# Out projection run once for each half of the tokens in a fused encoder layer

## What is computed

```python
def layer(h, attend, conv_state, w_in, w_out, ...):
    ...
    mix = jnp.concatenate([group_rms_norm(attn, g_attn_out, HEAD_DIM),
                           group_rms_norm(gate_b * conv_y, g_conv_out, CONV_GROUP)], axis=-1)
    h = h + rms_norm(jnp.einsum('bte,ed->btd', mix, w_out), g_post_mix)
    xf = rms_norm(h, g_pre_ffn)
    ff = jax.nn.silu(jnp.einsum('btd,df->btf', xf, w_gate)) * jnp.einsum('btd,df->btf', xf, w_up)
    h = h + rms_norm(jnp.einsum('btf,fd->btd', ff, w_down), g_post_ffn)
```

## Time and profile before

| what | us |
|---|---|
| median of 3 runs | 2453.63 (2452.96 to 2456.07) |
| profiled execution, its own time | 2450.74 |
| span in its trace | 2449.0 |
| TensorE busy | 2374.5 (97%) |
| VectorE busy | 1541.6 (63%) |
| ScalarE busy | 1011.0 (41%) |
| GpSimd busy | 81.9 (3%) |

### The profile page before, as it was taken

One profiled execution on the slowest core, in us unless ns is written; L12 is line 12 of the kernel. 1 busy time (PEld: TensorE's weight loads), 2 busy tenths in 40 slices (PEclk: granted clock), 3 DMA queues, 4 the chain that ended last, 5 costly groups with the idle time before them and its releaser, 6 DMA issues.

```text
span 2449.0 us, 42232 instructions
## 1 busy us (share of the span) xinstructions
PE 2374.5 (97%) x18280; PEld 2334.6 (95%) x18280; DVE 1541.6 (63%) x1778; ACT 1011.0 (41%) x1245; POOL 81.9 (3%) x143
## 2 busy tenths in 40 slices
PE   8999999999999996699999999999999899999998
PEld 7999999999999995699999999999999899999998
DVE  5323333343434225877777777777777688888887
ACT  6345444432333223444444444444444333333346
POOL 0000000000002110000000000000000000000002
PEclk9999999999999998799999999999999999999999
DMA  7222322222324331234445444444445666645562
GB/s 234 84 75 70 97 77 79 74 87 87 87 81 146 99 104 73 75 130 133 154 135 168 136 154 149 132 155 134 154 134 168 246 210 231 231 143 156 183 204 87
DMA packets 325916, 327.93 MB, mean 134 GB/s; under 512 B 8508, under 2 KB 282324, under 8 KB 325604
## 3 DMA queue, kind: packets, MB, share of 16 engines
q1 hardware_dynamic: 299264, 275.57, 35.9%
q10 hardware_dynamic: 26468, 49.67, 5.5%
HBM read 264.20 MB, written 61.00 MB: 133 GB/s over the span
## 4 chain that ended last, share of the span: by engine, by line
PE 90%; DVE 5%; DMA 2%; ACT 2%; issue 1%; SPq 0%; POOL 0%; ACTq 0%; DVEq 0%; POOLq 0%
PE ps L955 37%; PE ps L438 30%; PE ps L1012 17%; PE ps L722 4%; DMA ff_lo_scr<-hid_lo 2%; PE ps L666 1%; DVE xs L1800 1%; DVE t_lo L1778 1%; DVE misc L1804 0%; DVE panel L1792 0%; DVE wide L1768 0%; DVE misc L1772 0%; ACT xs L1350 0%; DMA panel<-in_w_down_dram 0%; DMA misc<-in_x_sample_dram 0%
## 5 line engine op out<-in xcount | busy, mean ns | idle before, releaser
L955 PE MATMUL ps<-xs,t_hi 128*128 128x272 f32 x4928 | 940.6, 291 | 33.0 <-DVE xs L1800 19.1
L955 PEld LDWEIGHTS ps<-xs,t_hi 128*128 128x128 f32 x4928 | 781.1, 190 | 34.6 <-issue 32.2
L955 PE MATMUL ps<-xs,t_lo 128*128 128x272 f32 x2464 | 716.8, 291 | 0.0
L1778 DVE TENSOR_TENSOR t_lo<-panel,t_hi 128x1024 fp32r<-128x1024 f32 (+1 forms) x405 | 485.5, 1199 | 228.3 <-ACT t_hi L1343 225.3
L1343 ACT CAST t_hi<-panel 128x1024 fp32r<-128x1024 f32 (+1 forms) x405 | 413.4, 1021 | 455.1 <-PE ps L1012 241.9
L1012 PE MATMUL ps<-xd,t_hi 128*128 128x272 f32 x2464 | 470.4, 290 | 14.3 <-DVE y_left L1949 8.2
L955 PEld LDWEIGHTS ps<-xs,t_lo 128*128 128x128 f32 x2464 | 467.3, 190 | 0.0
L438 PE MATMUL ps<-act_hi,w_hi 128*128 128x272 f32 (+1 forms) x2048 | 435.4, 294 | 3.1 <-DVE act_lo L1615 1.9
L438 PE MATMUL ps<-act_lo,w_hi 128*128 128x272 f32 (+1 forms) x2048 | 426.9, 290 | 0.0
L438 PE MATMUL ps<-act_hi,w_lo 128*128 128x272 f32 (+1 forms) x2048 | 426.5, 289 | 0.0
L1012 PEld LDWEIGHTS ps<-xd,t_hi 128*128 128x128 f32 x2464 | 390.7, 190 | 15.5 <-issue 15.4
(11 more groups left out here) (183 smaller groups left out, 1728.4 us busy)
## 6 DMA issues: line engine op xcount, KB each, us to landing
w_raw<-in_w_in_dram SPq DMA_DIRECT2D x96, 512.0 KB, 3.8
panel<-in_w_up_dram SPq DMA_DIRECT2D x44, 1024.0 KB, 5.6
panel<-in_w_gate_dram SPq DMA_DIRECT2D x43, 1024.0 KB, 5.1
panel<-in_w_down_dram SPq DMA_DIRECT2D x32, 1024.0 KB, 5.9
ff_hi_scr<-hid_hi SPq DMA_DIRECT2D x22, 952.0 KB, 4.5
ff_lo_scr<-hid_lo SPq DMA_DIRECT2D x22, 952.0 KB, 7.4
w_raw<-in_w_out_dram SPq DMA_DIRECT2D x32, 512.0 KB, 3.9
xd<-ff_hi_scr ACTq DMA_DIRECT2D x28, 544.0 KB, 8.0
```

The source lines that it names most:

```text
L955: mm = nc.tensor.matmul(out, w[:, k, :], xs[:, x, part, k, :], start=begins and k == 0 and w is hi and part == 0, stop=k == KH - 1 and w i ...
L1778: V.tensor_tensor(tile_of(t_lo, i), raw_tile(i), tile_of(t_hi, i).bitcast(F32), ALU.subtract)\
```

## The change

The out projection runs once for tokens 0 to 271 and then once for tokens 272 to 543. Every weight tile of w_out is loaded, cast and split twice (64 tiles), and a tile now serves 24 matmuls. The split mix lies in new buffers by half (`mx_hi`, `mx_lo`); the second half's is made while the first pass runs (`mix_high_late`, `mix_rest_late`). Output chunks use one of four banks in turn. While the second pass runs, the first half's norm, residual, squares and second norm are made, and A11 and A12 are split. The squares of h of the first half are folded by VectorE from 16 chunks to one ahead of one matmul; ScalarE's queue stores h. At the end of the second pass four products whose inputs are of the first half (B11 and B21 of steps 0 and 1) are made, with weight tiles that come through the ring of w_out as tiles 64 to 67. Steps 0 and 1 skip these two products.

S1 and S2 get raw buffers of their own, and GpSimd makes S3 and S4; the sums are gated by `s_pool`. `xs` is a list with a new order in memory (`XS_AT`), since S1's and S4's places overlap buffers that must be free first, and `xd` slots are permuted alike (`XD_AT`). In the down projection the last pair's first product goes into the gate buffer, VectorE's wait for the earlier store comes after the rest of B22 of its first step, the last pair's sums, rounding and rest move, and its store comes ahead of a panel load.

```diff
-    OUT_T = 2 * KC
+    OUT_T = 4 * KC + 4
...
+        mx_hi, mx_lo = ([sb_at(f"mx_{part}{t}", 17408 * (2 * p + t), [P, KC, TH], F32R) for t in range(2)]
+                        for p, part in enumerate(("hi", "lo")))
+        XS_AT = {A11: 0, A12: 2, S2: 1, S3: 3, S1: 4, A22: 5, S4: 6}
+        xs = [sb_at(f"xs{x}", 17408 * XS_AT[x], [P, 2, KH, TH], F32R) for x in range(7)]
+        s2_raw = sb_at("s2_raw", 69632, [P, KH, TH])
+        s1_raw = sb_at("s1_raw", 112640, [P, KH, TH])
...
+        XD_AT = [0, 1, 4, 5, 2, 3, 6, 7, 8, 9, 10, 11]
...
             sp.dma_start(resid, h_scr).then_inc(h_loaded, 16)
-            for q in range(2, KC // 2):
+            for q in range(2, KC):
                 load_out(q)
+            for k in range(PRE):
+                load((4, KC, T_OUT), k, gate_up[k // 2][:, TK * (k % 2):TK * (k % 2 + 1), 0:P])
...
+                if step == LAST + 3:
+                    store_hidden(FF // 2 - 1)
                 load_panel(step, 1)
-                if step > 3 and step % 2 == 0 and step // 2 - 2 < FF // 2:
+                if step > 3 and step % 2 == 0 and step // 2 - 2 < FF // 2 - 1:
                     store_hidden(step // 2 - 2)
...
+            for e in range(2, 2 * KC):
+                if e >= 4:
+                    pe.wait_ge(out_copied, e - 3)
+                if e == KC:
+                    pe.wait_ge(mix_late, 4)
+                for half in range(2):
+                    pe.wait_ge(lo_ready, T_OUT + 2 * e + half + 1)
+                    out_part(e, half, list(range(TK)))
+                if e == KC:
+                    out_sums(0)
+                if e == KC + 8:
+                    pe.wait_ge(h2_summed, 4)
+                    nc.tensor.matmul(ps[:, 5, 0:TH], neg1[:, :], h2_sq[0][:, 0, :], start=True, stop=True)\
+                        .then_inc(ms_ready, 1)
+            out_sums(1)
...
+            pe.wait_ge(ms_log, 3)
+            pre_product(0)
+            pre_product(1)
+            h2_sums(0)
+            pre_product(2)
+            for g in range(1, 4):
+                h2_sums(g)
+            pre_product(3)
...
+            for e in range(2 * KC):
+                t, n, q = e // KC, e % KC, e // 2
+                for half in range(2):
+                    ahead = 2 * e + half + LEAD
+                    if 2 * e + half >= 2 and ahead < OUT_T:
+                        round_weights((4, ahead // 4, T_OUT), ahead % 4)
+                if e in (3, 5, 7, 9):
+                    mix_high_late((e - 3) // 2)
+                if n == KC - 1:
+                    load_log_table(1)
+                act.wait_ge(chunk_done, CH_OUT + e + 1)
...
+                A(squares[n % 2][:, t * TH:(t + 1) * TH], ps[:, n % 4, 0:TH], ACT.Square).then_inc(sq_made, 1)
...
+            make_rstd(3)
+            for g in range(4):
+                square_stream(1, g)
+            load_log_table(2)
+            tile_high(ring(0, T2))
+            make_rstd(4)
+            act.wait_ge(product_done, PRE)
+            x_high(A22, x_block(KH, KH, 1), x_normed, 8)
+            x_high(S2, s2_raw[:, :, :], s_made, 2)
...
+                    act.wait_ge(xs_lo, 5)
+                    x_high(S1, s1_raw[:, :, :], s_pool, 2)
...
+                if e in (KC + 1, KC + 2):
+                    for g in range(2):
+                        scale_mix(0, 2 * (e - KC - 1) + g)
+                if e in (KC + 3, KC + 5):
+                    for g in range(2):
+                        add_mix(0, e - KC - 3 + g)
+                if e == KC + 7:
+                    fold_squares(0)
+                if e == KC + 8:
+                    for level in range(1, 4):
+                        fold_squares(level)
...
+            V.tensor_tensor(s1_raw[:, :, :], a21, a22, ALU.add).then_inc(s_made, 1)
+            dve.wait_ge(product_done, PRE)
+            dve.wait_ge(s_made, 1)
+            V.tensor_tensor(s2_raw[:, :, :], s1_raw[:, :, :], a11, ALU.subtract).then_inc(s_made, 1)
...
-                if step > 1:
+                if 1 < step < LAST:
                     dve.wait_ge(hid_stored, 32 * (step // 2))
...
+                if step == LAST:
+                    dve.wait_ge(hid_stored, 32 * (step // 2))
+                    dve.wait_ge(c12_up, FF // 2)
+                    V.tensor_copy(quarter(hid, 0, 1), quarter(gate, 0, 1))
...
+            pool.wait_ge(s_made, 1)
+            G.tensor_tensor(a21, a11, a21, ALU.subtract).then_inc(s_pool, 1)
+            pool.wait_ge(s_made, 2)
+            G.tensor_tensor(a12, a12, s2_raw[:, :, :], ALU.subtract).then_inc(s_pool, 1)
```

More of the change, by code:

```diff
@@ L945, in _, with out_part @@
-            mm.then_inc(ms_ready, 1)
+            def out_part(e, half, ks):
+                t, n = e // KC, e % KC
+                slot = (2 * e + half) % SLOTS
+                hi, lo = (w[:, slot, :].rearrange("p (k n) -> p k n", k=TK) for w in (w_hi, w_lo))
+                for k in ks:
+                    c = TK * half + k
+                    for w, part in ((hi, 0), (hi, 1), (lo, 0)):
+                        x = mx_lo[t][:, (c + 1) % KC, :] if part else mx_hi[t][:, c, :]
+                        mm = nc.tensor.matmul(ps[:, n % 4, 0:TH], w[:, k, :], x,
+                                              start=c == 0 and w is hi and part == 0,
+                                              stop=c == KC - 1 and w is lo, skip_group_check=True)
+                if ks[-1] == TK - 1:
+                    mm.then_inc((first_used, chunk_done)[half], 1)
@@ new lines, in _, with pre_product @@
+            out_sums(1)
+            def pre_product(k):
+                step, q = k // 2, k % 2
+                pe.wait_ge(lo_ready, T_OUT + 4 * KC + k + 1)
+                pe.wait_ge(xs_lo, 3 if q else 2)
+                pe.wait_ge(out_copied, 2 * KC)
+                hi, lo = (w[:, k, :].rearrange("p (k n) -> p k n", k=TK) for w in (w_hi, w_lo))
+                for c in range(KH):
+                    for w, part in ((hi, 0), (hi, 1), (lo, 0)):
+                        mm = nc.tensor.matmul(step_bank(step, "ac"[q]), w[:, c, :], xs[q][:, part, c, :],
+                                              start=c == 0 and w is hi and part == 0, stop=c == KH - 1 and w is lo,
+                                              skip_group_check=True)
+                mm.then_inc(product_done, 1)
@@ L963, in _ @@
                 for q in range(7):
-                    i = 7 * step + q
+                    if step < 2 and q <= B21:
+                        continue
+                    i = ring(step, q)
                     pe.wait_ge(tile_lo, i + 1)
@@ L1446, in _ @@
                     silu(quarter(gate, 1, 1), (c22_made, step + 1))
-                tile_high(ahead + 2)
+                tile_high(ring(step + 1, T2))
             def scale_chunk(c):
@@ new lines, in normalize, with x_rest @@
+            def normalize(t, c0, n):
+                for c in range(c0, c0 + n):
+                    x = resid[:, c, tokens_of(t)]
+                    last = V.scalar_tensor_tensor(out=x, in0=x, scalar=column(c + C_PREFFN), in1=rstd[:, tokens_of(t)],
+                                                  op0=ALU.mult, op1=ALU.mult)
+                last.then_inc(x_normed, 1)
+            def x_rest(x, made, block, k=0, n=KH):
+                dve.wait_ge(xs_hi, made)
+                V.tensor_tensor(xs[x][:, 1, k:k + n, :], block, xs[x][:, 0, k:k + n, :].bitcast(F32), ALU.subtract)\
+                    .then_inc(xs_lo, 1)
@@ L1775, in tile_rest @@
+            for ahead in range(4 * KC + LEAD, OUT_T):
+                rest_of_weights((4, ahead // 4, T_OUT), ahead % 4)
             def tile_rest(i):
@@ L1918, in _ @@
                     hidden_rest(step // 2 - 1)
-                tile_rest(7 * step + 6)
+                tile_rest(ring(step, B22))
                 if step == 0:
@@ L1923, in _ @@
                     c11(step)
-                tile_rest(ahead)
+                if step:
+                    tile_rest(ring(step + 1, B11))
                 combine(step + 1, T1)
@@ L1927, in _ @@
                 combine(step + 1, T2)
[L1928 removed]
+                if step:
+                    tile_rest(ring(step + 1, B21))
                 c21(step)
                 combine(step + 1, T3)
[L1931 removed]
+                tile_rest(ring(step + 1, T2))
             def take_down(d, q):
@@ L1985, in _ @@
                     combine(step + 1, T2)
-                    tile_rest(ahead + 1)
+                    tile_rest(ring(step + 1, B21))
                 take_down(d, T4)
@@ L1989, in _ @@
                     combine(step + 1, T3)
-                    tile_rest(ahead + 2)
+                    tile_rest(ring(step + 1, T2))
             take_down(DSTEPS - 1, B22)
```

416 lines of the change are left out of this document (217 added, 199 removed).

## The result

The changed kernel takes 2466.5 us (median of 5 runs, 2464.4 to 2470.1) against 2453.6 before (2453.0 to 2456.1): a ratio of 1.0053, 95% interval 1.0041 to 1.0065. It is 13 us slower, where 9.4 us faster was forecast. The measured time lies outside the range of 2424 to 2458.

What follows compares the result with a forecast made beforehand. TensorE, busy 97% of the span, was taken to bound the kernel. Out projection and transition +2.2, down projection -11.6, sum -9.4 on 2450.7: 2441.3, or 2444 as a median; range over all cases 2424 to 2458.

Steps and rivals of the forecast that it cites:

- supply term: Out projection, tiles 8 to 50: casts wait for loads through two raw slots, 6.5 us a pair against 6.05; +10.1.
- transition's sum: Out projection's end to steady products: 23.5 + 39.7 less products done and low clock, 52.6 us, gain -34.6.
- rival 1: Weights keep pace with TensorE in the out projection (at most 6.05 us a pair): 2425.7 us; chance 0.14.
- Start and load of h: Out projection's start costs +5.1 us; the load of h delays tile 8, costing +10.1.
- Rival 2: Inserted VectorE work adds in full to the out projection's weight supply loop: 17.8 us new, 2462 us; chance 0.13.
- Fold: TensorE waits behind chunk 24 of the out projection for VectorE's folded sums: +9.6 us (3.5 if weights run ahead).
- End to X: Out projection's end to the first half's second norm (X): last square at about 3.7 us, X at 23.5.
- X to steady products: Second norm's start to steady products: GpSimd's S3 and S4 at 7.0 us each, first product X + 17.4, end X + 39.5.
- Down projection: Its start: two TensorE holes shrink, together -11.6 us (-15 to -4).
- first hole: Down projection's start: VectorE no longer stands for an earlier hidden pair's store; -9.6 us, as little as -4.
- second hole: Down projection, two steps later: wait behind the last pair's store, now moved ahead of a panel load; -2 (bounds +5, -5).
- Rival 3: Down projection: the panel behind the store lands only at 2000, +4.9 instead of -2; 2451 us; chance 0.13.

Runs made afterwards that it cites:

- experiment 5: Changed kernel with a third raw slot for the out projection's weight tiles from tile 8 on: 2439.6 us, ratio 0.9942 to the kernel before.
- experiments 1 to 3: Changed kernel with S3 and S4 on VectorE: alone 2461.1 us; plus two unused GpSimd subtractions 2468.1; plus two unused GpSimd copies instead 2466.5.
- experiments 5, 7, 10: Changed kernel with third raw slot: alone 2439.6 us; with h in eight pieces 2428.2; with these, later fold matmul, S3/S4 on VectorE, store behind panel 2414.1.
- experiment 8: Kernel before with only the start of the down projection changed, the last pair's store ahead of the panel load: 2448.2 us, ratio 0.9975.
- experiment 9: Kernel before with only the start of the down projection changed, the last pair's store behind the panel load: 2441.9 us, ratio 0.9956.

## Why the prediction was wrong, step by step

The forecast of -9.4 and the profiled +15.8 are 25.2 apart. The terms account for 24.1 of it: 2.6 in the projection, 4.4 up to X, 8.1 from X to steady products, 5.6 at the down projection, and 3.4 in the tail, which is no part of the change. The step that failed most is the one that put GpSimd's sums at no more than 1.7 us of VectorE's time; the runs show 9.2. The prediction's own additions hold but for slips of 0.2 to 1.1 us: the supply term is 9.5 + 1 = 10.5 and not 10.1, the transition's sum has 39.7 where its last step is 39.5, and rival 1's end comes out at 955.3 and not 956.4.

*Start and load of h: right.* The first pair was done at about 755 instead of 758.4, h was issued at 757.84 (forecast 761.1), tile 8 was cast at 774.35 (forecast 778.3), 16.5 after it against the forecast's 17.2. TensorE's hole is 9.50, against 10.1.

*Weight supply: mechanism right, term too small.* The casts wait for loads, as named, and undisturbed pairs take 6.2 to 6.4 us; the pairs with the longest work put in take 7.5 to 9.0. But the mean from tile 10 to tile 52 is 6.79 a pair, (923.17 - 780.52) / 21, at the edge of my bound of 6.8, where I took 6.5: work put in between cost about 0.3 a pair more. It is 6 us over the stage, most of which the earlier start gave back. Rival 2, the insertions in full, did not come: about 6 of its 17.8 us did, and that its 2462 lies nearest to the measured 2466.5 is luck. The fit of the Trainium skill that the prediction sets beside this loop (DMA: Bandwidth & Descriptors, Anatomy of one DMA) is given there for DMAs that GpSimd issues, while SyncE issues these loads; their median from issue to landing is 4.0 us in the changed kernel, and the prediction was right to go by the measured gap. Rival 1 needed a faster loop, and experiment 5 shows what it would have been worth: 2439.6, not 2425.7, as the fold and the transition still stood there.

*Fold: right in kind, 6.6 to 10.5 of wait against 9.6.* The wait is 6.64 here and 8.66 to 10.48 in experiments 1 to 3, with the same projection. It is shorter here because TensorE came to it later: tile 49 ahead of it, after a wait of 2.60, took 4.81 us at a clock of 0.65 instead of 3.02. The projection's end was missed by 2.6 of 39.4.

*End to X: the choice between two values fell wrong.* I gave the last square a delay of 0.5 to 7.1 and took 3.7. With weights still late, the row of TensorE's matmul on it is:

```profile
979.44 1.27 PE L963 MATMUL ps<-w_raw,neg 128*128 128x272 f32 x2 [5.00 <-ACT w_raw L1428]
```

That is 5.6 after the end, which is 1.9 of the 4.4. Another 1.4 is ScalarE's cast of one more weight tile, which waited for its load and stands ahead of the rstd: from the last square to the rstd it is 2.63 us here and 1.23 in experiment 5. The other 1.1 is in neither. X came at +27.9, not +23.5; where weights are in stock (experiments 5, 7, 10) it is +21.5. The prediction had said that the last 14 tiles would be in stock, and used a middle value all the same.

*X to steady products: the step that failed most.* The prediction costed GpSimd's sums at 7.0 each because "VectorE never rests there", and put the price on GpSimd alone. For VectorE's own three operations up to the first product it took 9.0, that is 1.7 more than 3 x 2.42; they took 16.4. Experiments 1 to 3 show that a two-input operation of VectorE and one of GpSimd take turns: two operations of VectorE became 7.0. From X to steady work it was 47.6 us instead of 39.5. That S4 still ended near its forecast (X + 23.3 against X + 22.4) is luck: GpSimd's second sum took 6.91 because it waited for VectorE, and the first only 4.76.

The trace of the kernel before showed it already. The earlier trace rows has the same GpSimd sum at 1362 at the least and 1876 at the most, and I read the larger as a slowed engine. Its timeline, with VectorE's copy-out of a chunk, which reads the matmul's output:

```profile
786.52 1.88 POOL L2012 TENSOR_TENSOR buf_g<-buf_g,buf_e 128x544 f32<-128x544 f32 x1 [17.31 <-ACT buf_e L1152]
...
787.10 0.78 DVE L1754 TENSOR_SCALAR wide<-ps,cols 128x544 f32<-128x544 f32 x1
```

The sum starts while VectorE's rest of the earlier trace rows runs from 785.96 to 787.19. What is left of that rest, 0.67, and 1.37 alone are 2.04, where 1.88 came. VectorE's next rest, at 787.80, takes 1.69: 0.60 until the sum's end at 788.40, and 1.23, are 1.83. So the waiting of both engines could be read there to within 0.2 us, and the copy-out between them was not held.

The Trainium skill (SBUF — State Buffer, SBUF: two separate sides) states this: the pair of ports that VectorE and GpSimd share is an exclusive lock, taken for a whole instruction, and the other engine "fully blocks"; it holds for a VectorE instruction with two inputs in SBUF beside a GpSimd one that reads SBUF. The runs agree: 7.02 us instead of 2.42 beside a sum of 4.76, and 4.24 beside a copy of 2.00. The prediction drew on the Trainium skill's advice to use VectorE for such work (GPSIMD Engine Reference, Engine selection) and missed this. That advice pointed the right way too: with S3 and S4 on VectorE the median fell by 5.4.

*Down projection: one half right, the other half of the wrong sign.* The first hole went nearly as forecast: a wait of 1.62 is left, and the take-down of B11 is what is late next. 46 us behind its first xd matmul TensorE has done 350 matmuls where it had done 280, which at 0.126 us each is 8.8 of the 9.6. At the second hole I took -2 between bounds of +5 and -5, with two microseconds of the panel's delay as slack. The panel was issued at 1991.12 and cast at 2006.43; TensorE stood 5.27 instead of 4.42, and the window from 1990 to 2019 has 161 matmuls, where full pace gives 230. The second hole costs 2.9 more than before, 4.9 above my -2. In all -6.0 in the trace, -5.2 in experiment 8, instead of -11.6. With the order of the store undone (experiment 9) it is -11.4 by the medians and -10.1 in the trace: most of the shortfall of this term, if not all, is the store ahead of the panel. Rival 3 had the mechanism, at 6.9 above my term for the second hole; 4.9 came.

*What a better forecast would have been.* With turns on the shared engines (+8), the late end of the last square (+4) and rival 3's sign (+6), the same sum gives +8.6, where the trace has 12.4 up to the tail and the medians 12.9; the rest is the projection (2.6) and 1.1 that I can't place. These three are fitted after the result, so that they nearly add up is no test of them.

## What to carry to other kernels

Before work is moved from VectorE to GpSimd "because GpSimd is idle", add its full duration on GpSimd to VectorE's path wherever both would run at the same time: it isn't taken off. That is shown for VectorE operations with two inputs in SBUF. When a stage's loads double, take the loop through its buffers (load, cast, rest, next load) from the timeline and compare it with the consumer's pace; the busy shares here said 36 and 48 of 169 and hid a loop that was 4% too slow, and one more 512 KB slot was worth 27 us. A gain that a version loses can stand in pieces: here the change was 13 us slower and, with five small repairs found by its own waits, 39 us faster. Of these 39, the start of the down projection gives 11.4 by itself in the kernel before (experiment 9), with no pass by halves.

## What the runs showed of the hardware

A two-input VectorE operation of 2.42 us took 6.1 to 7.0 beside a two-input sum of GpSimd and 4.2 beside a GpSimd copy of 2.00; GpSimd's sum of 2176 elements took 3.8 to 4.8 when it began first and 6.9 when VectorE was at work. A VectorE operation of 0.78 us that reads the matmul's output took no longer beside such a sum. With a transfer of 4.6 MB issued just ahead of it, a 512 KB tile could be cast only 16.5 us after that issue, where such loads take 4.0 us at the median, and the same bytes in eight pieces among weight loads with three slots cost TensorE no wait of 0.8 us. The last part of the kernel, transposes and row sums at the very end, ran 26 us at full clock or 27 to 31 with a mean granted clock of 0.82 to 0.93, though no kernel changed it; single profiles shouldn't be compared to 3 us without looking at that clock.
